# Cached values loaded page by page from the cache, and index scores moved two tiles behind their queries

## The reference

```python
h = rmsnorm(x)
q, k, v, iq, ik, iw, u = split(h @ W_in)
scores = sum over 16 heads of relu(iq . ik / 8) * iw / 4     # index scores
idx = top_k(scores, 68 for the prompt, 256 for a sample)
a = softmax(q . k[idx]) @ v[idx]                             # samples: k, v, ik from a paged cache
p = causal pooling of u over windows 2, 4, 8, 16, mixed by pool_w
x = x + rmsnorm([a ; p] @ W_o)
x = x + rmsnorm((silu(gate) * val) @ W_down)                 # gate, val: causal conv of rmsnorm(x) @ W_up
```

## Time and profile before

| | |
|---|---|
| median of 3 runs | 1183.36 us |
| the profiled execution | 1183.83 us |
| its span, first to last instruction | 1182.0 us |
| TensorE busy | 1155.7 us (98%) |
| VectorE busy | 806.9 us (68%) |
| ScalarE busy | 531.5 us (45%) |
| GpSimd busy | 55.3 us (5%) |
| mean granted TensorE clock | 0.994 |
| DMA | 238.76 MB, 202 GB/s |

### The profile page before, as it was taken

The page is one execution under the profiler, slowest core; times in us unless marked ns, Lnnn a source line. Parts: engine busy times, 40 slices in busy tenths (PEclk is TensorE's granted clock), DMA queues, the critical chain, the costliest instruction groups (busy, mean ns, idle before and its releaser), DMA issues.

```text
span 1182.0 us, 25876 instructions
## 1 busy us (share of the span) xinstructions
PE 1155.7 (98%) x9172; PEld 1119.0 (95%) x9172; DVE 806.9 (68%) x1523; ACT 531.5 (45%) x753; POOL 55.3 (5%) x66
## 2 busy tenths in 40 slices
PE   8989999999998999999999999999999999999998
PEld 7879999867897899999999999999999999999997
DVE  4775798876478877777777777777777544444443
ACT  7342333434245655454545454545455433333332
POOL 4710000000003100000000000000000000000000
PEclk9999999999999999999999999999999999999999
DMA  8977878768852565545555555555556866666651
GB/s 310 317 262 246 257 244 304 256 211 274 306 202 91 184 206 164 189 164 188 167 185 169 184 171 181 171 183 170 183 168 185 264 178 179 180 180 185 181 166 74
DMA packets 81080, 238.76 MB, mean 202 GB/s; under 512 B 9440, under 2 KB 28992, under 8 KB 78704
## 3 DMA queue, kind: packets, MB, share of 16 engines
q1 hardware_dynamic: 75152, 225.40, 59.5%
q10 hardware_dynamic: 4480, 9.01, 2.2%
q0 software_dynamic: 1408, 3.84, 1.0%
HBM read 231.64 MB, written 24.16 MB: 216 GB/s over the span
## 4 chain that ended last, share of the span: by engine, by line
PE 89%; DVE 4%; DMA 2%; SPq 2%; issue 1%; ACT 1%; POOL 0%; DVEq 0%; ACTq 0%; POOLq 0%
PE bank L1475 28%; PE bank L1476 28%; PE bank L1478 28%; DMA raw<-in_w_in 2%; DVE part L1344 1%; DMA cache_ring<-kscr 1%; DVE lo L443 1%; PE bank L1692 1%; SPq L486 1%; SPq L485 1%; DVE h_lo L1349 1%; PE bank L1668 0%; PE bank L1844 0%; SPq L484 0%; PE bank L1657 0%
## 5 line engine op out<-in xcount | busy, mean ns | idle before, releaser
L1475 PE MATMUL bank<-h_hi,hi 128*128 128x266 f32 (+1 forms) x2096 | 604.1, 288 | 1.5 <-DVE lo L443 1.5
L1478 PE MATMUL bank<-h_hi,lo 128*128 128x266 f32 (+1 forms) x2096 | 602.8, 288 | 0.0
L1476 PE MATMUL bank<-h_lo,hi 128*128 128x266 f32 (+1 forms) x2096 | 602.1, 287 | 0.0
L443 DVE TENSOR_TENSOR lo<-raw,hi 128x1024 fp32r<-128x1024 f32 (+2 forms) x362 | 431.6, 1198 | 208.1 <-ACT hi L435 194.5
L435 ACT ACTIVATE hi<-raw 128x1024 fp32r<-128x1024 f32 (+2 forms) x362 | 373.5, 1034 | 287.8 <-PE bank L1478 265.0
L1475 PEld LDWEIGHTS bank<-h_hi,hi 128*128 128x128 f32 x2096 | 397.4, 190 | 6.0 <-issue 3.9
L1476 PEld LDWEIGHTS bank<-h_lo,hi 128*128 128x128 f32 x2096 | 396.0, 189 | 0.1
L1478 PEld LDWEIGHTS bank<-h_hi,lo 128*128 128x128 f32 x2096 | 395.7, 189 | 0.0
L1476 PE MATMUL bank<-g_lo,hi 128*128 128x264 f32 x704 | 200.5, 285 | 0.0
L1478 PE MATMUL bank<-g_hi,lo 128*128 128x264 f32 x704 | 199.6, 284 | 0.0
L1475 PE MATMUL bank<-g_hi,hi 128*128 128x264 f32 x704 | 199.4, 283 | 0.0
(11 more groups left out here) (279 smaller groups left out, 612.6 us busy)
## 6 DMA issues: line engine op xcount, KB each, us to landing
raw<-in_w_up SPq DMA_DIRECT2D x176, 512.0 KB, 3.8
raw<-in_w_in SPq DMA_DIRECT2D x56, 512.0 KB, 5.0
raw<-in_w_down SPq DMA_DIRECT2D x64, 448.0 KB, 3.5
raw<-in_w_o SPq DMA_DIRECT2D x32, 512.0 KB, 4.8
raw<-in_w_down SPq DMA_DIRECT2D x32, 512.0 KB, 3.8
kscr<-in_cache_k SPq DMA_DIRECT2D x64, 128.0 KB
vscr<-in_cache_v SPq DMA_DIRECT2D x64, 128.0 KB
mixed<-kscr SPq DMA_DIRECT2D x8, 512.0 KB, 7.2
```

Of the source, the lines that this page charges most:

```text
L443: ops.tensor_tensor(lo[:, s, 0:width], raw[:, s, 0:width], hi[:, s, 0:width].bitcast(F32), ALU.subtract).then_inc(done, 1)
L1475: mm(out, w_hi, x_hi[:, k, first:], start=(opens and done == 0), stop=False)
L1476: mm(out, w_hi, x_lo[:, k, first:], start=False, stop=False)
L1478: last = mm(out, w_lo, x_hi[:, k, first:], start=False, stop=(closes and done == total))
```

## The change

1. **Values.** `vscr` and its 64 copies are gone. `load_v` reads the page number and loads that page of the cache into SBUF, eight register loads and eight DMAs of 128 KB for a sample. SyncE does samples 2, 3, 5 and 6, GpSimd samples 0, 1, 4 and 7, behind the gathers of index keys and before its three last DMAs. The waits are those of before; `sample_values` waits for all eight pages of a sample.
2. **Page copies out of the index stage.** SyncE issues the weight loads of the eight query tiles first, then four key pages, then three behind the loads of each projection tile.
3. **Order of the index stage.** `iq` has four slots, tile 3 has bank 5. TensorE does tile 3 before `weights_turned`, then scores 0 and 2, and from tile 4 on the scores of tile t−2 after tile t. Score 12 follows the last query tile, score 14 and that of the last rows the first projection tile; the sum of the last rows and the sample scores follow the second, the sample sums the third. ScalarE and VectorE follow that order.
4. **VectorE in the projection.** Index sums 10 to 15 stand among the first two tiles, `prompt_round` starts in the third; two `sort_round`s stand in each of tiles 4 to 7.
5. **Loads held back.** The mask `S` is loaded after x, the gathers of index keys start after the first query tile, the two loads for pooling come after the sample relus. ScalarE rounds the first query chunk after all of `h_hi`.

```diff
+        return bank[(3, 5)[t - 2] if t in (2, 3) else (T_IQ + t) % 2]
...
+        def load_v(eng, b):
+            if b < GROUPS:
+                eng.wait_ge(kq_used, 4)
+            elif b == GROUPS:
+                eng.wait_ge(score_done, NU)
+            elif b == GROUPS + 1:
+                eng.wait_ge(pv_done, NU)
+            else:
+                eng.wait_ge(spv_done, 1)
+            for g in range(PAGES):
+                n = PAGES * b + g
+                page = eng.value_load(ptrow[0:1, n:n + 1], min_val=0, max_val=a["cache_v"].shape[0] - 1)
+                eng.dma_start(value_slot(b)[:, g, :], a["cache_v"][page]).then_inc(v_loaded[b], 16)
...
-            load_in(0, C_IQ, 0)
+            for t in range(8):
+                load_in(0, C_IQ + 2 * t, t)
             sp.wait_ge(pt_loaded, 48)
-            def paced_in(i, t, n0, n, r):
...
+            for n in range(4):
+                key_page(n)
+            def paced_in(i, t, n0):
+                load_in(i, C_IQ + 2 * t, 2 * i + t)
+                for k in range(3):
+                    key_page(6 * i + n0 + k)
+            with sp.Fori(0, 10) as i:
+                paced_in(i, 8, 4)
+                paced_in(i, 9, 7)
...
+                    load_v(sp, u - 3)
             load_wo(17)
-            load_v(5)
+            load_v(sp, 5)
             load_wo(18)
-            load_v(6)
-            load_v(7)
+            load_v(sp, 6)
...
+            pool.wait_ge(x_loaded[len(X_PARTS) - 2], 16)
             pool.dma_start(S[:, :], a["causal"]).then_inc(s_loaded, 16)
             pool.wait_ge(kix_ready, 1)
+            pool.wait_ge(chunk_used, C_IQ + 2)
...
+            for b in (0, 1, 4, 7):
+                load_v(pool, b)
...
-                if k == 13:
-                    hi_chunk(ae, 0, C_IQ)
                 nc.scalar.activation(h_hi[:, k, :], x0[:, k, :], ACT.Copy,
                                      scale=par[:, G1 + k:G1 + k + 1]).then_inc(h_hi_ready, 1)
+            hi_chunk(ae, 0, C_IQ)
...
+            for j in range(4, 7):
+                hi_chunk(ae, 0, C_IQ + j)
             root(1)
-            ae.wait_ge(h_lo_ready, KM)
-            ae.dma_start(partf[:, 0:2048], a["pool_w"]).then_inc(poolw_loaded, 16)
-            ae.dma_start(partf[:, 2048:2048 + 960], a["state_pool"]).then_inc(poolw_loaded, 16)
+            hi_chunk(ae, 0, C_IQ + 7)
...
+            for t in range(4, 9):
+                hi_tile(C_IQ + 2 * t)
+                for n in range(0 if t == 4 else 2 * t - 8, 2 * t - 6):
+                    relu_head(n, n % 2)
+            for h in range(10, 14):
                 relu_head(h, h % 2)
-                if h < 14:
-                    hi_chunk(ae, 0, C_PROJ + h - 10)
-                if h == 13:
-                    ae.wait_ge(score3_done, 1)
-                    for n in range(2):
-                        nc.scalar.activation(relu3[n], bank[3 + 2 * n][:, 0:TP], ACT.Relu,
-                                             scale=IDX_SCALE).then_inc(relu3_ready, 1)
-            hi_chunk(ae, 0, C_PROJ + 4)
-            hi_chunk(ae, 0, C_PROJ + 5)
+            hi_tile(C_PROJ + 2)
+            for h in range(14, 16):
+                relu_head(h, h % 2)
...
+            lo_chunk(dve, nc.vector, lo_dve, 0, C_IQ + 6)
             inv_rms(1)
+            lo_chunk(dve, nc.vector, lo_dve, 0, C_IQ + 7)
...
             for t in range(8):
-                if t in range(2, 8):
+                if t >= 3:
                     lo_chunk(dve, nc.vector, lo_dve, 0, C_IQ + 2 * t + 2)
                     lo_chunk(dve, nc.vector, lo_dve, 0, C_IQ + 2 * t + 3)
-                if t >= 2:
-                    index_sum(2 * t - 4)
-                    index_sum(2 * t - 3)
+                    index_sum(2 * t - 6)
+                    index_sum(2 * t - 5)
                 if t:
                     index_queries(t)
...
             for t in range(U0, U0 + 8):
-                if t:
-                    low_halves(t + 1)
+                if t == 0:
+                    index_sum(10)
+                    index_sum(11)
+                low_halves(t + 1)
+                if t < 2:
+                    index_sum(2 * t + 12)
+                    index_sum(2 * t + 13)
                 if t == 2:
+                    index_sum_3()
+                if t == 3:
                     sample_lists()
-                else:
+                elif t >= 2:
                     prompt_round(next(rounds_p))
+                if t >= 4:
+                    sort_round(2 * t - 8)
+                    sort_round(2 * t - 7)
...
-                if h < 2:
+                if h < 4:
                     prompt_round(next(rounds_p))
-                if h == 2:
+                if h == 4:
                     prompt_mask()
-                if h in range(3, 7):
+                if h in (5, 6):
...
+            def index_scores(h):
+                pe.wait_ge(iq_ready, h // 2 + 1)
+                if h >= 2:
                     pe.wait_ge(relu_ready, h)
...
+            q_idx_tile(0, 3)
             weights_turned()
-            for t in range(2):
-                pe.wait_ge(iq_ready, t + 1)
-                index_scores(2 * t, t)
-            with pe.Fori(1, 3) as i:
-                q_idx_pair(i, i)
-            pe.wait_ge(iq_ready, 6)
-            q_idx_tile(0, 7)
-            pe.wait_ge(iq_ready, 7)
-            index_scores(12, 0)
-            pe.wait_ge(iq_ready, 8)
-            for n in range(2):
-                last = mm(bank[3 + 2 * n][:, 0:TP], iq3[:, P * n:P * n + P], ikT[0:IDX_DIM, 0:TP], start=True, stop=True)
-            last.then_inc(score3_done, 1)
-            index_scores(14, 1)
-            pe.wait_ge(relu3_ready, 2)
-            for n in range(2):
-                last = mm(misc[0:16, 128:128 + TP], iwq3[:, n, :], relu3[n], start=(n == 0), stop=(n == 1))
-            last.then_inc(sum3_done, 1)
+            index_scores(0)
+            index_scores(2)
+            for t in range(4, 8):
+                pe.wait_ge(iq_ready, t - 3 if t < 6 else t - 1)
+                q_idx_tile(0, t)
+                index_scores(2 * t - 4)
+            index_scores(12)
...
+            index_scores(14)
+            for n in range(2):
+                last = mm(bank[3 + 2 * n][:, 0:TP], iq3[:, P * n:P * n + P], ikT[0:IDX_DIM, 0:TP], start=True, stop=True)
+            last.then_inc(score3_done, 1)
+            proj_tile(0, 1, T_PROJ + 1)
+            pe.wait_ge(relu3_ready, 2)
+            for n in range(2):
+                last = mm(misc[0:16, 128:128 + TP], iwq3[:, n, :], relu3[n], start=(n == 0), stop=(n == 1))
+            last.then_inc(sum3_done, 1)
...
-            proj_tile(0, 1, T_PROJ + 1)
+            proj_tile(0, 2, T_PROJ + 2)
             pe.wait_ge(srelu_done, 3)
             pe.wait_ge(sum3_used, 1)
...
-            with pe.Fori(0, 5) as i:
+            proj_tile(0, 3, T_PROJ + 3)
+            with pe.Fori(1, 5) as i:
...
-                    pe.wait_ge(v_loaded[GROUPS * r + j], 16)
+                    pe.wait_ge(v_loaded[GROUPS * r + j], 16 * PAGES)
```

More of the change, by code:

```diff
@@ L260, in build_program @@
     x1 = mixed[:, :].rearrange("p (k t) -> p k t", k=KM)
-    iq = short[:, 0:2 * T].rearrange("p (h t) -> p h t", h=2)
+    iq = short[:, 0:4 * T].rearrange("p (h t) -> p h t", h=4)
     relu = short[:, 1120:1120 + 768].rearrange("p (r s) -> p r s", r=2)
@@ L480, in _, with key_page @@
                     load(0, C_IK + j, a["w_ik"][:, j * 8 * IKW:(j + 1) * 8 * IKW], 8 * IKW)
-            def pages(n):
+            def key_page(n):
                 page = sp.value_load(ptrow[0:1, bass.ds(n, 1)], min_val=0, max_val=a["cache_k"].shape[0] - 1)
                 sp.dma_start(kscr[n], a["cache_k"][page]).then_inc(scr_loaded, 16)
-                sp.dma_start(vscr[n], a["cache_v"][page]).then_inc(scr_loaded, 16)
             w_in = a["w_in"]
@@ L493, in load_in @@
                     load(r, cj + j, w_in[t, :, j * CW:(j + 1) * CW])
-            load_in(0, C_IQ, 0)
+            for t in range(8):
+                load_in(0, C_IQ + 2 * t, t)
             sp.wait_ge(pt_loaded, 48)
-            def paced_in(i, t, n0, n, r):
[L500 to L517, removed]
+            for n in range(4):
[7 more added lines that the diff above has]
+                paced_in(i, 9, 7)
+            k_src = kscr.rearrange("(b g) p e -> b p g e", b=DB)
             def load_k(r, c):
@@ L543, in _ @@
                 load_wo(n)
-            sp.wait_ge(scr_loaded, 2 * DB * PAGES * 16)
+            sp.wait_ge(scr_loaded, DB * PAGES * 16)
             sp.wait_ge(sidx_done, 1)
@@ L1526, in q_idx_tile @@
                         between()
-            def index_scores(h, p):
-                if not isinstance(h, int) or h >= 2:
+            def index_scores(h):
+                pe.wait_ge(iq_ready, h // 2 + 1)
+                if h >= 2:
                     pe.wait_ge(relu_ready, h)
@@ L1535, in index_scores @@
                         o = bank[2 + 2 * e][0:nq, A_AT[n]:A_AT[n] + nk]
```

(2 more changed lines are left out.)

70 lines of the change are left out of this document (19 added, 51 removed).

## The result

The changed kernel takes 1192.3 us (median of 4 runs, 1191.3 to 1193.4), the kernel before 1184.0 us beside it. The ratio is 1.0061, 95% interval 1.0050 to 1.0073: 0.6% slower (the two medians alone give 0.7%). The prediction, 1184.9 us against 1183.4, had the right side and missed 7.4 us of the time. 1192.3 lies 0.3 us above its range; the ratio applied to its own 1183.36 gives 1190.6, inside it.

A forecast was written before the change was run, and what follows sets the result against it. TensorE was taken as the bound, busy 1155.7 of 1182.0 us. 1183.83 − 4.6 (index stage) + 4.4 (value wait) + 1.7 (clock) = 1185.3 us, predicted as 1184.9 since that execution was 0.47 above the median; range 1178.5 to 1192.

The forecast's parts named there:

- Index stage: TensorE's waits and slow clock in the index stage: 10.3 us before, 6.1 after; gain 4.2, with 0.4 ahead 4.6 us.
- VectorE's rounds at nothing: Projection tiles: the moved maximum and sorting rounds just fit VectorE's waiting time, so they cost nothing.
- The values: Attention stage: TensorE waits 4.4 us for page-by-page values at the second product with values, plus 1.7 us of slow clock.
- the same 4.6 us earlier: Value stage: what starts the value loads and what reads them were both taken to come 4.6 us earlier.
- Part 3: Value loads in the attention stage: page-by-page loading was to cost a 4.4 us TensorE wait and 1.7 us of clock.
- the sum: Whole kernel: 1183.83 − 4.6 + 4.4 + 1.7 = 1185.3 us, predicted as 1184.9 us against the runs' median.
- part 1: Index stage on TensorE: the same matmuls in another order, with less idle time and slow clock, gain 4.6 us.
- Rival (c): Index stage gives nothing back: it gains only 1 us and the values cost 6.1, 1188.5 us; chance 0.10.
- rival (b): Values come much later, on GpSimd: TensorE waits 11.9 us, clock costs 3, 1193.7 us; chance 0.20.

The follow-up runs named there:

- e2: The kernel before with only the values' part: value copies dropped, values loaded page by page on SyncE and GpSimd; 1190.8 us, ratio 1.0049.
- e7: The changed kernel with key and value page copies kept, paced as before, and one value load a list from the copies; 1184.8 us, ratio 1.0000.
- e6: The changed kernel with value list 6 alone in one load from fixed cache pages, still on SyncE; 1191.8 us, ratio 1.0045.
- e12: The changed kernel with value lists 5 and 6 each in one load from fixed cache pages, on SyncE; 1188.6 us, ratio 1.0028.
- e1: The changed kernel with each value list in one load from fixed cache pages, all on SyncE, without page look-up; 1184.4 us, ratio 0.9996.

## Why the prediction missed by seven microseconds

**Index stage: right in size, half right in cause.** Tile 0 at 18.13 (said: by 18.4), the waits 1.59 and 2.08 (1.4 and 2.0), clock 0.80 over 7.4 us (1.5 us; 1.7 said), none near 80 us, 1.05 for the relu (1.0), fourth projection tile 4.9 us earlier at its start, 4.7 at its end (4.6). But the gain was credited to the new order alone. The prediction had seen why tile 7 is late, the copies on SyncE, and still priced their removal at nothing of its own; e2 shows that they alone give 4.1. The sum didn't suffer, because the two gains don't add.

**VectorE's rounds at nothing:** right; the 4.7 us stand unchanged from the end of that tile to 232 us.

**The values: the right wait, the size inside the ends.** Said 4.4 us and 1.7 of clock, measured 5.7 and 1.7. SyncE's last page is issued at 312.1, or 311.5 when the 0.6 us are taken off by which TensorE is later than before just ahead: 311.5 was forecast. That agreement is partly luck: the first page went out at 273.75, not 272.4, and a page took 1.14 us, not 1.17. What was mis-sized is its landing, 3 us, measured 4.8. GpSimd's page was 1.14 us (0.55 and 0.59 of gap), not 1.28, and its last landing 4.3, not 5, so that it was 3 us earlier than forecast and not the last. By the page "DMA: Bandwidth & Descriptors" of the Trainium skill, in its section on the anatomy of one DMA from GpSimd, the estimate was 2.3 us to landing and, with it, SyncE as the one that decides. The trace agrees on who is last and not on the landing: the medians on GpSimd's queue are 3.5 us for lists 0 and 1, 5.7 for list 4 and 4.2 for list 7. The terms were taken one queue at a time; that with both together the DMA engines move 266 GB/s where list loads move 338 was in no term. That this makes what comes behind them land late fits the traces and isn't shown by a run of its own.

**The step that failed: "the same 4.6 us earlier".** Part 3 and the sum carried the gain of part 1 to the end, on the ground that tiles follow each other up to the attention stage and that the chain is TensorE's. The attention stage has a wait of 2.55 us of its own, at 236.95 in the trace of before, which was not among the rows; behind it and behind the key pages at 259 us the clock fell in the changed kernel, which cost 3.0 and 1.65 us, and the wait on the key pages was 0.65 us longer: 5.3 us in all. That took back the 4.7 us of gain and 0.6 more. e7 shows that without page loads of values: 3.8 us early at 233, no gain at the end. All this is one trace against one; if the kernel before loses clock there too in most of its executions, the change costs less than these 3.0 us against them. Adding these 5.3 and the 1.3 of the wait to 1185.3 gives 1191.9, against 1191.7 of the profiled execution. Rival (c), the index stage giving nothing back, came nearest in effect, with another mechanism and 3.6 us where 5.3 were lost; rival (b) came nearest in time, 1193.7 us, by a wait of 11.9 us that was 5.7.

## What to carry to other kernels

A gain far ahead of a stage is worth only what that stage's own waits let through: list the idle stretches behind the change too, and ask at each what the clock does if it falls there. Loading a list in pages is paid in the queue's time a page and, as far as the traces tell, once more in DMA engines that move less while buffers are free; copies made ahead, while the queue has time, were cheaper here than page loads at the point of use, unless the weight loads stand behind them. Where two parts of a change cure the same wait, try each alone before either is credited. And see, by its clock among the other executions, whether a profiled execution is typical before a stage is explained by it.

## What the runs showed of the hardware

- A page load costs its queue nearly the same on both engines: 1.14 us on GpSimd and 1.1 to 1.2 us on SyncE (8.31 us for eight), though the issue alone is 0.55 and 0.33 us.
- With two such queues the 16 DMA engines carry 266 GB/s in a stretch in which list loads carry 338 (after and before, 275 to 295 us). A 1 MB load of list 6 behind them lands after 13.6 us (e6) and 14.8 (e12); the last two lists land after 8.2 and 10.6 us in the kernel before and 7.2 and 9.8 in e1, though an earlier list of e1 took 13.5.
- An idle stretch of 2.55 us ahead of small products let TensorE's clock fall to 1.2 GHz in ten of ten profiles of changed kernels and left it at 2.4 in the one of the kernel before; with 0 to 0.3 us of idle in the same place it was whole in three of three, one of them the kernel before with the products.
